# Second feed-forward down projection: seven half-depth products for each block of two token tiles and two column blocks, in place of eight

## The chip, the cores and the metric

The kernel runs on one core of one Trainium2 chip. The metric is the device time of one execution in microseconds (us); lower is better. All data is float32, and each float32 matmul of the program stands in the trace as two records on TensorE (PE), so 704 matmuls are 1408 records.

## The reference, cut to what matters

The program is a two-layer block with a modulation vector, two kinds of mixers and a convolved feed-forward network. The change touches only the feed-forward network of the second layer (`l = 1`), where the context rows are no longer needed and 512 tokens are left:

```
D_MODEL = 1024
SEQ = 512
D_FF = ((8 * D_MODEL // 3 + 127) // 128) * 128        # 2816, 22 tiles of 128

def conv_ffn(h, w_up, conv_w, w_down):
    a, g = jnp.split(dwconv(h @ w_up, conv_w), 2, axis=-1)
    return (jax.nn.silu(g) * a) @ w_down

x = x + mx[:, :, 5] * rmsnorm(conv_ffn(hx, ffn_w_up[l], ffn_conv[l], ffn_w_down[l]), norm_g[l, 3])
```

The product `(silu(g) * a) @ w_down` is the down projection: 512 tokens by 2816 hidden rows by 1024 columns. After it come the norm of each token's row, the gate and the addition to `x`, and `x` is the output.

## The kernel before

The kernel is written engine by engine: each stage is a block with one program for each engine, and the engines wait for each other by semaphores. There is no scheduler, so the order of the calls in the source is the order on the engine. At the end of a block all engines meet at a barrier (its instructions carry the line of the `with ... nc.Block()`, L1369 for `mix_and_up`). The last two stages are `mix_and_up(c, 1, 0, "cd_out", ...)`, which ends with the up projection, and `down_and_store(c)`.

**Up projection.** The hidden rows are made in 22 pairs (a gate tile and a value tile of 128 hidden rows each). Pairs 2 to 21 are made with seven products of half depth (`UpPairs`), and each goes through DVE (VectorE) in one iteration of the loop over `n`: `join_weights(n + 1)` makes four sums of the next pair's weights (L1639 to L1644), two `convolve` calls finish the pair before (L362, L366), seven additions gather the seven products (L1648, from PSUM), and `multiply(n - 1)` forms the finished hidden tile (L1617). After the loop, DVE still convolves and multiplies pair 21. ACT (ScalarE) copies, scales and takes the silu. `hidden[:, n, :]` holds 768 columns for each tile, of which the second layer uses 512.

**Down projection.** `Down` runs 32 units: for two groups of token tiles, (0, 1) and (2, 3), for eight column blocks of 128, for the two tiles of the group. A unit (L1916) is 22 matmuls with a hidden tile as the stationary operand and 128 columns of weights as the moving one, summed in one PSUM bank of 128 columns. ACT copies the even units out (L1937) and DVE the odd ones (L1943); ACT squares each (L1957). At the half DVE sums the squares of tiles 0 and 1 (L1822), ACT takes the root (L1826), and DVE divides, gates and adds these rows (L1833, L1835, L1838); at the end the same is done for tiles 2 and 3.

**Weights.** All weights come through a ring of four slots, filled by SP (SyncE) in the order of `c.plan`. A load waits until the products that used its slot are done (`c.used`). For the down projection each column block takes two slots, the upper and the lower half of the 2816 rows (11 tiles of 128 columns), so that two column blocks are in the ring at a time. The first four loads are issued by the stage before.

Of the kernel before, what the change touches and what calls it, by code (L numbers as in the profile page):

```python
# [326 lines left out]
def plan_all(c):  # L327
# [1015 lines left out]
def mix_and_up(c, l, z, name, src):  # L1343
# [25 lines left out]
    with st, nc.Block() as block:  # L1369
# [6 lines left out]
        strassen, copied, whole, weights_joined, tokens_joined = \  # L1376
            (sem(n) for n in ("strassen", "copied", "whole", "weights_joined", "tokens_joined"))

        @block.sync
        def _(sp):  # L1380
# [180 lines left out]
        def _(dve):  # L1561
# [106 lines left out]
            for n in range(begun, FT):  # L1668
# [62 lines left out]
def ffn_hidden(c):  # L1731
    return c.arena[:, 0:FT * N_ALL].rearrange("p (k t) -> p k t", k=FT), FT * N_ALL
# [504 lines left out]
                nc.vector.tensor_copy(v_[:, t, :], c.ps[:, (0, 2, 4, 5)[t % 4], 0:128]).then_inc(v_dve, 1)  # L2237


def down_and_store(c):  # L2240


    nc = c.nc
    st, sem = stage(c)
    rows = RowChain(c, sem, Down.CHUNKS)
    down = Down(c, 1, [(0, 1), (2, 3)], sem, rows)
    n_units, half = len(down.units), len(down.units) // 2
    with st, nc.Block() as block:
        @block.sync
        def _(sp):  # L2250
            c.stream(sp, "down1")
            for t in range(TX):
                sp.wait_ge(rows.added, t + 1)
                sp.dma_start(c.a["out"][0, t * 128:(t + 1) * 128, :], c.x[:, t, :]).then_inc(c.stored, 16)
            sp.wait_ge(c.stored, 16 * TX)

        @block.tensor
        def _(pe):
            for n in range(n_units):
                down.unit(pe, n)  # L2260

        @block.scalar
        def _(act):
            for n in range(n_units):
                if n % 2 == 0:
                    down.keep_act(act, n)
                if n:
                    down.square(act, n - 1)
                if n == half + 1:
                    for i in range(2):  # L2270
                        rows.branch_root(act, i)
            down.square(act, n_units - 1)
            for i in range(2, TX):
                rows.branch_root(act, i)

        @block.vector
        def _(dve):
            for n in range(n_units):
                if n == half:
                    for i in range(2):  # L2280
                        rows.sum_squares(dve, i, half)
                if n == half + 2:
                    for i in range(2):
                        rows.add(dve, i)
                if n % 2:
                    down.keep_dve(dve, n)
            for i in range(2, TX):
                rows.sum_squares(dve, i, n_units)
            for i in range(2, TX):
                rows.add(dve, i)  # L2290

# [1068 lines left out]
```

## Time and profile before

| | |
|---|---|
| median of three runs | 2490.5 us (2490.29 to 2492.77) |
| the profiled execution | 2486.43 us, of which the span of its instructions is 2484.6 us |
| PE busy | 2269.7 us, 91% of the span |
| DVE busy | 1112.6 us, 45% |
| ACT busy | 546.1 us, 22% |
| L1916, both down projections | 405.2 us of PE, 3520 records |
| the second down projection | from 2315.30 us, for 159.65 us, 1408 records |

Times in the rows count from the start of the span. A matmul's record has a duration that overlaps with the next one's, so the pace of PE is read from distances between events and not from durations. "PEclk" or the number before the DMA share in a row of windows is the granted clock of TensorE: 1.00 is 2.4 GHz and 0.50 is 1.2 GHz. "Idle before <-releaser" says how long an engine stood before an instruction and what ended that.

### The profile page before, as it was taken

What the parts mean: (1) busy time and instruction counts of PE and PEld (TensorE: products, weight loads), DVE (VectorE), ACT (ScalarE), POOL (GpSimd) and SP (SyncE); (2) the same over time, 40 slices, a digit from 0 to 9 for tenths busy, and PEclk for the clock granted to TensorE, in tenths of its full rate; (3) what the DMA queues carried; (4) which work ended last, traced back from release to release, by engine and by line L of the source; (5) the groups of instructions that cost most, each with busy time, mean ns of one, the idle gap of its engine ahead of it and who ended that gap; (6) DMA issues with size and microseconds to landing.
All of it is one profiled execution on the core that took longest, in us unless ns stands there. A gap on an engine that the chain in (4) does not pass through costs nothing. (4 is left out here: it accounts for less than half of the span.)

```text
span 2484.6 us, 39011 instructions
## 1 busy us (share of the span) xinstructions
PE 2269.7 (91%) x16786; PEld 1677.7 (68%) x16786; DVE 1112.6 (45%) x2140; ACT 546.1 (22%) x1241; POOL 229.9 (9%) x303
## 2 busy tenths in 40 slices
PE   3999989979993999999989999998887899999998
PEld 1557655558882865555559999545454588888898
DVE  2124822257761255666660003232676536677211
ACT  3102722321212231111110002111452132111110
POOL 2000100027760000000000000000210000000000
PEclk9999989989996999999999999999798899999999
DMA  8351001000003012122134556411000213333454
GB/s 327 113 192 35 1 18 51 0 1 4 4 4 136 5 47 68 51 63 56 52 80 151 160 168 202 142 60 27 29 1 18 68 35 85 85 85 85 126 155 128
DMA packets 236301, 193.55 MB, mean 78 GB/s; under 512 B 5395, under 2 KB 220130, under 8 KB 235938
## 3 DMA queue, kind: packets, MB, share of 16 engines
q1 hardware_dynamic: 223266, 145.53, 20.3%
q0 software_dynamic: 11776, 42.27, 4.8%
q8 instruction: 133, 2.18, 0.4%
q10 hardware_dynamic: 1088, 3.26, 0.3%
q14 instruction: 38, 0.31, 0.0%
HBM read 188.94 MB, written 2.10 MB: 77 GB/s over the span
## 5 line engine op out<-in xcount | busy, mean ns | idle before, releaser
L1454 PE MATMUL banks<-mem 128*128 128x384 f32 (+1 forms) x2296 | 622.1, 433 | 0.0
L1454 PEld LDWEIGHTS banks<-mem 128*128 128x128 f32 x2296 | 434.3, 189 | 187.3
L1916 PE MATMUL banks<-mem 128*128 128x128 f32 x3520 | 405.2, 277 | 13.9 <-PEq L1369 12.6
L1916 PEld LDWEIGHTS banks<-mem 128*128 128x128 f32 x3520 | 400.6, 194 | 23.7 <-issue 22.4
L2001 PE MATMUL banks<-mem 128*128 128x512 f32 x400 | 191.4, 609 | 6.0 <-issue 6.0
L1943 DVE COPY mem<-banks 128x128 f32<-128x128 f32 x40 | 11.7, 293 | 350.5 <-PE banks L1916 350.4
L1394 PE MATMUL banks<-mem 128*128 128x256 f32 x640 | 143.2, 384 | 13.2 <-PEq L616 11.1
L1648 DVE TENSOR_TENSOR mem<-mem,banks 128x384 f32<-128x384 f32 (+1 forms) x287 | 131.1, 487 | 38.5 <-PE banks L1454 35.7
L1394 PEld LDWEIGHTS banks<-mem 128*128 128x128 f32 x640 | 122.6, 193 | 32.1 <-issue 14.0
L921 PE MATMUL banks<-mem 64*64 64x64 f32 x3840 | 127.4, 220 | 18.5 <-DVE mem L1197 11.4
L921 PEld LDWEIGHTS banks<-mem 64*64 64x64 f32 x3840 | 119.7, 136 | 28.8 <-DVE mem L1197 13.7
L697 PE MATMUL banks<-mem 128*128 128x512 f32 x256 | 130.9, 592 | 1.2 <-PEq L415 1.2
L2001 PEld LDWEIGHTS banks<-mem 128*128 128x128 f32 x400 | 76.3, 194 | 76.1 <-issue 70.8
L1524 ACT ACTIVATE mem<-mem 128x768 f32<-128x768 f32 (+1 forms) x44 | 32.5, 739 | 342.4 <-DVE mem L366 342.4
L362 DVE SCALAR_TENSOR_TENSOR mem<-banks,mem 128x511 f32<-128x511 f32 (+1 forms) x44 | 28.0, 663 | 172.0 <-ACT mem L726 107.5
L1639 DVE TENSOR_TENSOR mem<-mem 128x512 f32<-128x512 f32 x41 | 28.4, 694 | 168.1 <-DMA mem<-in_ffn_w_up 168.1
L1533 ACT ACTIVATE mem<-mem 128x768 f32<-128x768 f32 (+1 forms) x82 | 66.0, 829 | 145.5 <-DVE mem L1648 145.5
L1937 ACT ACTIVATE mem<-banks 128x128 f32<-128x128 f32 x40 | 11.1, 278 | 362.3 <-PE banks L1916 350.2
L698 PEld LDWEIGHTS banks<-mem 128*128 128x128 f32 x256 | 48.4, 189 | 61.7 <-issue 61.7
L366 DVE SCALAR_TENSOR_TENSOR mem<-mem 128x511 f32<-128x511 f32 x124 | 78.2, 659 | 2.9
L362 DVE SCALAR_TENSOR_TENSOR mem<-mem 128x511 f32<-128x511 f32 x124 | 77.9, 657 | 0.5 <-ACT mem L1533 0.5
L698 PE MATMUL banks<-mem 128*128 128x256 f32 x256 | 76.2, 378 | 0.0
(343 smaller groups left out, 2743.9 us busy)
## 6 DMA issues: line engine op xcount, KB each, us to landing
mem<-in_ffn_w_up SPq DMA_DIRECT2D x88, 512.0 KB, 4.3
mem<-in_ffn_w_down SPq DMA_DIRECT2D x64, 704.0 KB, 6.6
mem<-in_w_mod POOLq DMA_DIRECT2D x40, 1024.0 KB, 7.5
mem<-in_ab_w_in SPq DMA_DIRECT2D x14, 1024.0 KB, 5.3
mem<-in_w_mod SPq DMA_DIRECT2D x8, 1024.0 KB, 14.1
mem<-in_cd_w_in SPq DMA_DIRECT2D x8, 1024.0 KB, 5.6
mem<-in_ab_w_out SPq DMA_DIRECT2D x4, 1024.0 KB, 9.0
mem<-in_cd_w_out SPq DMA_DIRECT2D x4, 1024.0 KB, 9.0
```

What stands on the lines that cost most here:

```text
L362: step = v.scalar_tensor_tensor(out[:, 1:n], src[:, 0:n - 1], tap(0), out[:, 1:n], ALU.mult, ALU.add)
L366: step = v.scalar_tensor_tensor(out[:, 0:n - 1], src[:, 1:n], tap(2), out[:, 0:n - 1], ALU.mult, ALU.add)
L697: nc.tensor.matmul(c.ps[:, x, :], w[:, k, :], ht[:, k, 0:N_X], start=k == 0, stop=k == KT - 1)
L698: last = nc.tensor.matmul(c.ps[:, z, 0:N_Z], w[:, k, :], ht[:, k, N_X:N_ALL], start=k == 0, stop=k == KT - 1)
L921: last = mm(c.ps[pa, LEVEL[i], fr], lhs[pa, fr], rhs[pa, fr], start=True, stop=True)
L1394: last = nc.tensor.matmul(c.ps[:, unit_banks[n % 4], 0:256], src[:, k, t * 128:(t + 1) * 128], w[:, k, :], start=k == 0, stop=k == KT - 1)
L1454: last = nc.tensor.matmul(fast.out(i, name), weights[:, k, :], tokens[:, k, :], start=k == 0, stop=k == 3)
L1524: f(gbuf[:, 0:n_all], gbuf[:, 0:n_all], ACT.Silu).then_inc(gated, 1)
L1533: f(dst[:, 0:n_all], fast.raw(n, half), ACT.Identity, scale=middle_tap(n, half)).then_inc(drained, 1)
L1648: v.tensor_tensor(to, one, fast.out(i, name), ALU.add).then_inc(whole, 1)
L1916: last = c.nc.tensor.matmul(c.ps[:, n % self.n_banks, 0:128], hidden[:, k, t * 128:(t + 1) * 128], w, start=k == 0, stop=k == FT - 1)
L2001: last = c.nc.tensor.matmul(c.ps[:, self.bank(n)[0], :], w[:, k, :], ht[:, k, 0:N_X], start=k == 0, stop=k == KT - 1)
```

## The change

`down_and_store` uses a new class `DownPairs` in place of `Down`. Its unit of work is a step: two token tiles (a group) by two column blocks of 128. For the four 128x128 blocks of the output it makes seven products instead of eight, each over half of the 22 hidden tiles (11), from sums of blocks of the hidden rows and sums of blocks of the weights. There are eight steps, four for each group. A step has two parts, of 6 and 5 of the 11 tiles, and a part's weights take two slots of the ring: now 256 columns wide and 6 or 5 tiles deep. Part by part, DVE makes the four weight sums (`join`), PE runs the seven products (`step`), and after the second part ACT keeps the first product (`keep_first`) and DVE adds up the others (`gather`). ACT takes four squares for each step. The sums of the hidden rows (`join_hidden`) are made in the stage before, 44 operations of 256 columns on DVE, as the hidden tiles arise.

```diff
-    c.plan("down1", down(a["ffn_w_down"][1]) * 2)
+    c.plan("down1", [ktiles(a["ffn_w_down"][1])[:, 11 * h + lo:11 * h + hi, i:i + 256]
+                     for i in range(0, D, 256) for lo, hi in DownPairs.PARTS for h in range(2)] * 2)
...
+            def join_hidden(n):
+                k = n - FT // 2
+                if z == 0 and k >= 0:
+                    (a11, a21), (a12, a22) = (DownPairs.tokens(c, row) for row in (k, n))
+                    s1, s2, s4 = DownPairs.sums(c, k)
+                    dve.wait_ge(done, n + 1)
+                    v.tensor_tensor(s1, a21, a22, ALU.add).then_inc(hidden_joined, 1)
+                    dve.wait_ge(hidden_joined, 4 * k + 1)
+                    v.tensor_tensor(s2, s1, a11, ALU.subtract).then_inc(hidden_joined, 1)
+                    v.tensor_tensor(a21, a11, a21, ALU.subtract).then_inc(hidden_joined, 1)
+                    dve.wait_ge(hidden_joined, 4 * k + 2)
+                    v.tensor_tensor(s4, a12, s2, ALU.subtract).then_inc(hidden_joined, 1)
...
                 add_up(i, value_rows[0], value_rows[0], "p4")
+                join_hidden(n - 1)
             convolve_pair(FT - 1, 0)
             convolve_pair(FT - 1, 1)
             multiply(FT - 1)
+            join_hidden(FT - 1)
...
+class DownPairs:
+    PARTS = ((0, 6), (6, 11))
+    ORDER = ("p1", "p2", "p6", "p5", "p7", "p3", "p4")
+    FREED = {"p6": 1, "p2": 2, "p7": 3, "p5": 5, "p3": 6, "p4": 7}
+    STEPS, PER_GROUP = 8, 4
...
+        for q in range(2 * self.STEPS):
+            for h in range(2):
+                c.used[self.lo + 2 * q + h] = (self.product, 7 * q + 7)
...
+    def join(self, dve, q):
+        v = self.c.nc.vector
+        b11, b12, b21, b22, t1, t2, t4 = self.parts(q)
+        for h in range(2):
+            self.c.arrived(dve, self.lo + 2 * q + h)
+        v.tensor_tensor(t1, b12, b11, ALU.subtract).then_inc(self.joined, 1)
+        dve.wait_ge(self.joined, 4 * q + 1)
+        v.tensor_tensor(t2, b22, t1, ALU.subtract).then_inc(self.joined, 1)
+        v.tensor_tensor(b12, b22, b12, ALU.subtract).then_inc(self.joined, 1)
+        dve.wait_ge(self.joined, 4 * q + 2)
+        v.tensor_tensor(t4, b21, t2, ALU.subtract).then_inc(self.joined, 1)
...
+    def step(self, pe, s):
...
+            def times(name, rows, weights):
+                if s and part == 0:
+                    if name == "p1":
+                        pe.wait_ge(self.copied, s)
+                    else:
+                        pe.wait_ge(self.whole, 7 * (s - 1) + self.FREED[name])
+                for k in range(lo, hi):
+                    last = c.nc.tensor.matmul(self.out(name), rows(k)[:, group, :], weights[:, k - lo, :],
+                                              start=k == 0, stop=k == 10)
+                last.then_inc(self.product, 1)
+
+            for h in range(2):
+                c.arrived(pe, self.lo + 2 * q + h)
+            times("p1", lambda k: self.tokens(c, k)[0], b11)
+            times("p2", lambda k: self.tokens(c, 11 + k)[0], b21)
+            pe.wait_ge(self.joined, 4 * q + 2)
+            times("p6", lambda k: self.sums(c, k)[1], t2)
+            times("p5", lambda k: self.sums(c, k)[0], t1)
+            pe.wait_ge(self.joined, 4 * q + 4)
+            times("p7", lambda k: self.tokens(c, k)[1], b12)
+            times("p3", lambda k: self.sums(c, k)[2], b22)
+            times("p4", lambda k: self.tokens(c, 11 + k)[1], t4)
...
+    def keep_first(self, act, s):
+        act.wait_ge(*self.done(s, "p1"))
+        self.c.nc.scalar.activation(self.place(s, 0, 0), self.out("p1"), ACT.Copy).then_inc(self.copied, 1)
+
+    def gather(self, dve, s):
+        y11, y12, y21, y22 = (self.place(s, b, j) for b in range(2) for j in range(2))
+
+        def add_up(to, one, name):
+            dve.wait_ge(*self.done(s, name))
+            self.c.nc.vector.tensor_tensor(to, one, self.out(name), ALU.add).then_inc(self.whole, 1)
+
+        dve.wait_ge(self.copied, s + 1)
+        add_up(y12, y11, "p6")
+        add_up(y11, y11, "p2")
+        dve.wait_ge(self.whole, 7 * s + 1)
+        add_up(y21, y12, "p7")
+        dve.wait_ge(self.whole, 7 * s + 3)
+        add_up(y22, y21, "p5")
+        add_up(y12, y12, "p5")
+        dve.wait_ge(self.whole, 7 * s + 5)
+        add_up(y12, y12, "p3")
+        add_up(y21, y21, "p4")
...
         @block.scalar
         def _(act):
...
+            for s in range(steps):
+                down.keep_first(act, s)
+                if s == half:
                     for i in range(2):
                         rows.branch_root(act, i)
+                down.square(act, s)
...
         @block.vector
         def _(dve):
...
+            down.join(dve, 0)
+            for s in range(steps):
+                down.join(dve, 2 * s + 1)
+                if s == half:
                     for i in range(2):
+                        rows.sum_squares(dve, i, 4 * half)
                     for i in range(2):
                         rows.add(dve, i)
+                down.gather(dve, s)
+                if s + 1 < steps:
+                    down.join(dve, 2 * s + 2)
```

On DVE, the end of the up projection reads as follows before the change: the last seven additions of pair 21 (L1648, around one L1617 for pair 20), then the convolution and the product of pair 21, and then the barrier.

```order
L1648 TENSOR_TENSOR mem<-mem,banks 128x256 x2
L1617 TENSOR_TENSOR mem<-mem 128x512
L1648 TENSOR_TENSOR mem<-mem,banks 128x256 x5
L362 SCALAR_TENSOR_TENSOR mem<-mem 128x511
L366 SCALAR_TENSOR_TENSOR mem<-mem 128x511
L362 SCALAR_TENSOR_TENSOR mem<-mem 128x511
L366 SCALAR_TENSOR_TENSOR mem<-mem 128x511
L1617 TENSOR_TENSOR mem<-mem 128x512
```

After the change DVE has, at the same place (all lines of this function stand one later), two groups of four sums of hidden rows, L1665 to L1670:

```order
L1649 TENSOR_TENSOR mem<-mem,banks 128x256 x5
L1665 TENSOR_TENSOR mem<-mem 128x256
L1667 TENSOR_TENSOR mem<-mem 128x256
L1668 TENSOR_TENSOR mem<-mem 128x2x128
L1670 TENSOR_TENSOR mem<-mem 128x256
L363 SCALAR_TENSOR_TENSOR mem<-mem 128x511
L367 SCALAR_TENSOR_TENSOR mem<-mem 128x511
L363 SCALAR_TENSOR_TENSOR mem<-mem 128x511
L367 SCALAR_TENSOR_TENSOR mem<-mem 128x511
L1618 TENSOR_TENSOR mem<-mem 128x512
L1665 TENSOR_TENSOR mem<-mem 128x256
L1667 TENSOR_TENSOR mem<-mem 128x256
```

The first group, for hidden tile 20, stands ahead of the last convolutions; the second, for tile 21, stands behind the last product and ahead of the barrier.

On DVE, in the middle of the down projection, the program before the change has nothing but copies around the rows of tiles 0 and 1:

```order
L1943 COPY mem<-banks 128x128 x8
L1822 TENSOR_REDUCE mem<-mem 128x1 x2
L1943 COPY mem<-banks 128x128
L1833 RECIPROCAL mem<-mem 128x1
L1835 SCALAR_TENSOR_TENSOR mem<-mem 128x1024
L1838 TENSOR_TENSOR mem<-mem 128x1024
```

After the change the rows of tiles 0 and 1 (L1840 to L1856) stand in step 4, between the weight sums of its second part (640 columns) and its `gather` (L2360), and the weight sums for step 5 (768 columns, L2304 on) stand behind both:

```order
L2309 TENSOR_TENSOR mem<-mem 128x640
L1840 TENSOR_REDUCE mem<-mem 128x1 x2
L1851 RECIPROCAL mem<-mem 128x1
L1853 SCALAR_TENSOR_TENSOR mem<-mem 128x1024
L1856 TENSOR_TENSOR mem<-mem 128x1024
L1851 RECIPROCAL mem<-mem 128x1
L1853 SCALAR_TENSOR_TENSOR mem<-mem 128x1024
L1856 TENSOR_TENSOR mem<-mem 128x1024
L2360 TENSOR_TENSOR mem<-mem,banks 128x128 x7
L2304 TENSOR_TENSOR mem<-mem 128x768
L2306 TENSOR_TENSOR mem<-mem 128x768
L2307 TENSOR_TENSOR mem<-mem 128x6x128
```

On PE the last stage is one kind of instruction, before and after, with fewer of them:

```order
-L1916 MATMUL banks<-mem 128x128 x704
+L2328 MATMUL banks<-mem 128x128 x616
```

Shape and operands of a matmul stay as they were.

## Rows read from the trace of the kernel before

**Rows 1.** The page's first line.

```profile
span 2484.6 us, 39011 instructions
```

**Rows 2.** Chain of waits that ended last: start us, us, what.

```profile
2315.30 159.65 PE banks L1916 x1408
...
2474.97 0.30 DVE mem L1943
...
2480.34 1.23 DVE mem L1838
```

**Rows 3.** Timeline of the down projection: start us, us, engine, line, operation.

```profile
2322.66 0.28 ACT L1937 ACTIVATE mem<-banks 128x128 f32<-128x128 f32 x1 [8.56 <-PE banks L1916]
...
2337.40 0.29 DVE L1943 COPY mem<-banks 128x128 f32<-128x128 f32 x1 [9.53 <-PE banks L1916]
```

**Rows 4.** Timeline where the up projection ends.

```profile
2269.70 40.37 PE L1454 MATMUL banks<-mem 128*128 128x256 f32 x186
...
2310.11 0.42 DVE L1648 TENSOR_TENSOR mem<-mem,banks 128x256 f32<-128x256 f32 x1 [1.24 <-PE banks L1454]
2310.45 0.75 DVE L362 SCALAR_TENSOR_TENSOR mem<-mem 128x511 f32<-128x511 f32 x1
...
2314.13 0.69 DVE L1617 TENSOR_TENSOR mem<-mem 128x512 f32<-128x512 f32 x1 [0.70 <-ACT mem L1524]
```

**Rows 5.** Windows there: us, busy PE, PEld, DVE, ACT, POOL, clock, DMA share, GB/s.

```profile
2313.00:2313.50 0.50, 0.00 (x0) 0.00 (x0) 0.43 (x1) 0.04 (x1) 0.00 (x0) 0.53 1.15 349
...
2319.50:2320.00 0.50, 0.50 (x4) 0.50 (x4) 0.00 (x0) 0.00 (x0) 0.00 (x0) 0.64 0.00 0
```

**Rows 6.** DVE groups by shape: count, busy us, mean ns of one, idle before.

```profile
L1648 DVE TENSOR_TENSOR mem<-mem,banks 128x256 f32<-128x256 f32 x140 | 53.5, 419 | 4.4 <-PE banks L1454 3.1
...
L1641 DVE TENSOR_TENSOR mem<-mem 128x512 f32<-128x512 f32 x41 | 28.4, 694 | 1.4
...
L1617 DVE TENSOR_TENSOR mem<-mem 128x768 f32<-128x768 f32 x22 | 21.1, 960 | 0.9 <-ACT mem L1524 0.9
```

**Rows 7.** Timeline of one iteration of the up projection, on DVE.

```profile
2279.67 0.69 DVE L1639 TENSOR_TENSOR mem<-mem 128x512 f32<-128x512 f32 x1 [3.12 <-DMA mem<-in_ffn_w_up]
...
2286.50 1.99 DVE L1648 TENSOR_TENSOR mem<-mem,banks 128x256 f32<-128x256 f32 x5
...
2291.70 0.69 DVE L1639 TENSOR_TENSOR mem<-mem 128x512 f32<-128x512 f32 x1 [3.20 <-DMA mem<-in_ffn_w_up]
2292.43 0.69 DVE L1641 TENSOR_TENSOR mem<-mem 128x512 f32<-128x512 f32 x1
2293.03 0.69 DVE L1642 TENSOR_TENSOR mem<-mem 128x512 f32<-128x512 f32 x1
```

**Rows 8.** Timeline of the rows' roots, at the half and at the end.

```profile
2402.35 1.28 ACT L1826 ACT_TABLE_LOAD   x1
...
2476.16 0.17 DVE L1833 RECIPROCAL mem<-mem 128x1 f32<-128x1 f32 x1 [0.20 <-ACT mem L1826]
```

**Rows 9.** A pair of weight loads: issue, windows; and all 28 loads of the stage.

```profile
2327.56 10.88 SPq L191 DMA_DIRECT2D mem<-in_ffn_w_down  x4
...
2333.00:2333.50 0.50, 0.50 (x7) 0.50 (x6) 0.00 (x0) 0.41 (x3) 0.00 (x0) 1.00 1.23 296
2333.50:2334.00 0.50, 0.50 (x7) 0.50 (x6) 0.00 (x0) 0.04 (x1) 0.00 (x0) 1.00 0.77 179
...
DMA to landing us min/median/max: 4.5/5.9/7.7
```

**Rows 10.** Two short stands of PE in the timeline, and windows behind them.

```profile
1482.79 3.50 PE L1916 MATMUL banks<-mem 128*128 128x128 f32 x18 [1.23 <-DVE mem L1759]
...
1483.50:1487.00 3.50, 3.50 (x20) 3.50 (x19) 0.00 (x0) 0.00 (x0) 0.00 (x0) 0.51 1.17 323
...
908.22 1.13 PE L1413 MATMUL banks<-mem 128*128 128x256 f32 x4 [2.12 <-ACT mem L1504]
...
906.00:910.00 4.00, 1.88 (x9) 1.60 (x9) 3.68 (x8) 2.17 (x7) 0.00 (x0) 1.00 0.02 4
```

More of the change, by code:

```diff
@@ L2237, in _, with __init__, tokens, sums @@
                 nc.vector.tensor_copy(v_[:, t, :], c.ps[:, (0, 2, 4, 5)[t % 4], 0:128]).then_inc(v_dve, 1)
+class DownPairs:
[3 more added lines that the diff above has]
+    STEPS, PER_GROUP = 8, 4
+    def __init__(self, c, sem, rows):
+        self.c, self.rows = c, rows
+        self.lo = c.range_of["down1"][0]
+        names = ("down_product", "down_copied", "down_whole", "down_joined")
+        self.product, self.copied, self.whole, self.joined = (sem(n) for n in names)
+        self.room = c.arena[:, FT * N_ALL:FT * N_ALL + 2 * 3 * 768].rearrange("p (b s n) -> p b s n", b=2, s=3)
+        for q in range(2 * self.STEPS):
+            for h in range(2):
+                c.used[self.lo + 2 * q + h] = (self.product, 7 * q + 7)
+    @staticmethod
+    def tokens(c, row):
+        pairs = ffn_hidden(c)[0][:, row, 0:N_X].rearrange("p (g b t) -> p g b t", g=2, b=2)
+        return pairs[:, :, 0, :], pairs[:, :, 1, :]
+    @staticmethod
+    def sums(c, k):
+        hidden = ffn_hidden(c)[0]
+        z = c.z.rearrange("p t d -> p (t d)")
+        o = _TABLE["cos"][0] + 256 * (k - 8)
+        last = z[:, 256 * k:256 * k + 256] if k < 8 else c.table[:, o:o + 256]
+        return [ap.rearrange("p (g t) -> p g t", g=2) for ap in (hidden[:, k, N_X:N_ALL], hidden[:, FT // 2 + k, N_X:N_ALL], last)]
+    def parts(self, q):
+        lo, hi = self.PARTS[q % 2]
+        n = hi - lo
+        (b11, b12), (b21, b22) = ([self.c.slot(self.lo + 2 * q + h, n, 256)[:, :, at:at + 128] for at in (0, 128)] for h in range(2))
+        t1, t2, t4 = (self.room[:, q % 2, s, 0:128 * n].rearrange("p (k n) -> p k n", k=n) for s in range(3))
+        return b11, b12, b21, b22, t1, t2, t4
+    def join(self, dve, q):
[9 more added lines that the diff above has]
+        v.tensor_tensor(t4, b21, t2, ALU.subtract).then_inc(self.joined, 1)
+    def out(self, name):
+        return self.c.ps[:, self.ORDER.index(name), 0:128]
+    def step(self, pe, s):
+        c, group = self.c, s // self.PER_GROUP
+        for part in range(2):
+            q = 2 * s + part
+            lo, hi = self.PARTS[part]
+            b11, b12, b21, b22, t1, t2, t4 = self.parts(q)
+            def times(name, rows, weights):
[19 more added lines that the diff above has]
+            times("p4", lambda k: self.tokens(c, 11 + k)[1], t4)
+    def place(self, s, b, j):
+        at = 256 * (s % self.PER_GROUP) + 128 * j
+        return self.rows.y[:, 2 * (s // self.PER_GROUP) + b, at:at + 128]
+    def done(self, s, name):
+        return self.product, 14 * s + 7 + self.ORDER.index(name) + 1
+    def keep_first(self, act, s):
[17 more added lines that the diff above has]
+        add_up(y21, y21, "p4")
+    def square(self, act, s):
+        for n, (b, j, ready) in enumerate(((0, 0, 2), (1, 1, 4), (0, 1, 6), (1, 0, 7)), 4 * s):
+            t, chunk = 2 * (s // self.PER_GROUP) + b, 2 * (s % self.PER_GROUP) + j
+            act.wait_ge(self.whole, 7 * s + ready)
+            if n:
+                act.wait_ge(self.rows.squared, n)
+            self.c.nc.scalar.activation(self.rows.junk, self.place(s, b, j), ACT.Square,
+                                        accum_out=self.rows.squares[:, t, chunk:chunk + 1]).then_inc(self.rows.squared, 1)
@@ L2245, in down_and_store @@
     rows = RowChain(c, sem, Down.CHUNKS)
-    down = Down(c, 1, [(0, 1), (2, 3)], sem, rows)
-    n_units, half = len(down.units), len(down.units) // 2
+    down = DownPairs(c, sem, rows)
+    half, steps = down.PER_GROUP, down.STEPS
     with st, nc.Block() as block:
@@ L2258, in _ @@
         def _(pe):
-            for n in range(n_units):
-                down.unit(pe, n)
+            for s in range(steps):
+                down.step(pe, s)
         @block.scalar
         def _(act):
[L2264 to L2269, printed above, removed]
+            for s in range(steps):
+                down.keep_first(act, s)
+                if s == half:
                     for i in range(2):
                         rows.branch_root(act, i)
-            down.square(act, n_units - 1)
+                down.square(act, s)
             for i in range(2, TX):
```

13 lines of the change are left out of this document (4 added, 9 removed).

## The prediction, made before the changed kernel ran

> **What bounds the kernel now.** I read the chain of waits first. Its last long piece is the whole second down projection: PE runs 1408 records from 2315.30 us for 159.65 us with nothing between them, and behind it stands a tail on DVE and ACT that ends at 2481.57 us [rows 2]. The span is 2484.6 us [rows 1]; the profiled execution took 2486.43 us and the median of the runs is 2490.5 us, so the profile lies 4.1 us below the median. The sum below is made on the profiled execution, and I carry the difference over to the median.
>
> Then the timeline inside the stage. DVE is idle for 9.53 of 9.83 us before each of its copies and ACT for 8.56 us before its first one, in both cases for PE [rows 3]. So PE sets the time of the stage and work taken from it is worth its whole length, as long as the new work on DVE does not make PE wait.
>
> The pace: DVE's copies at 2337.40 us [rows 3] and 2474.97 us [rows 2] are 28 units of 44 records apart, 137.57 / 1232 = 111.7 ns a record. The first unit took 7.36 us (2315.30 to 2322.66 [rows 2, 3]) where 44 records at that pace take 4.91 us: 2.45 us more. The reason is in the windows: PE stopped at 2269.70 + 40.37 = 2310.07 us [rows 4], the granted clock fell to its 1.2 GHz level soon after 2313.0 us, and came back to 2.4 GHz within 2319.5 to 2320 us [rows 5].
>
> **PE, removed.** 704 matmuls become 616, 88 fewer, or 176 records of the same shape. 176 x 111.7 ns = 19.65 us. Is the pace the same when PE changes bank and product every 5 or 6 matmuls and not every 22? The up projection changes every 4: its iterations start 12.03 us apart [rows 7] with 7 x 4 x 2 = 56 records of 256 columns, 214.8 ns each. Twice 111.7 would be 223. So changing products costs nothing that shows. I count **-19.65 us**. Its bounds are that price and, if each of the 112 products cost one more record's 0.11 us, 12 us less; the row of the up projection is near and excludes most of that.
>
> **DVE prices.** A 256-column TENSOR_TENSOR from PSUM takes 419 ns, one of 512 columns 694, of 768 columns 960 [rows 6]: 1.04 ns a column, so 640 columns take 827 and 256 from SBUF about 430. Starts lie 0.73 us apart where the second needs the first, 0.60 where it does not [rows 7]: the length plus 0.04, or less 0.09. A join of 768 columns then has its second sum ready after 1.00 + 0.96 = 1.96 us, and all four after 3.7 us. Four sums of hidden rows take 0.47 + 0.34 + 0.34 + 0.43 = 1.58 us, or move the next instruction by 1.49 us.
>
> **Sums of hidden rows.** Of the 11 groups, 9 stand at the end of an iteration of the up projection. DVE is idle there, for 3.12 and 3.20 us before `join_weights`, for the weights [rows 7]; 1.49 us fit, and cost nothing. Without that cover it would be up to 9 x 1.49 = 13.4 us. The last two have none. PE's last product ends at 2310.07 us; from its addition at 2310.11 us DVE works through the convolutions to the product at 2314.13 us, which ends at 2314.82 us [rows 4]; PE starts 0.48 us later [rows 2]. The group for tile 20 stands ahead of these convolutions (+1.49 us), the one for tile 21 behind the product (+1.58 us). **+3.07 us**, bounds 2.5 (nothing between sums) and 4. PE then stands 8.3 us instead of 5.2; the clock is down before it restarts either way, and I leave the 2.45 us as they are, bounds 1.7 and 3.2.
>
> **Start of the stage.** The first four loads are issued by the stage before, as now. DVE's first join has its second sum ready 1.96 us after the barrier; PE needs it after two products of 6 matmuls, 2.68 us at full clock and later at the low one. Nothing.
>
> **Each boundary between steps.** A part of 6 takes PE 7 x 6 x 0.2233 = 9.38 us, one of 5 7.82 us, a step 17.19 us. Let a step end at T. The last addition of `gather` needs the last product, so it starts at T + 0.02; the join of the next part 0 stands behind it, starts at about T + 0.23 (128 columns take 0.29, from L1943 [rows 3], less 0.09) and has its second sum at T + 2.19. PE asks for it at T + 2.68. The margin is 0.5 us, and all of the join that PE waits for is behind work that can't end before T. The third and fourth sums are there at T + 3.9 and PE asks at T + 5.4. The second part's join has 9.4 us. Nothing, but thinly.
>
> **Loads.** 32 loads and 22.5 MB, as before. A part-0 pair grows from 1.44 to 1.57 MB and is issued when the same slots' products end, with only the part of 5 (7.82 us) as cover; before, the cover was two units, 9.83 us. The pair issued at 2327.56 us flowed until about 2334.0 us, 6.4 us, at up to 296 GB/s; 0.13 MB more is 0.45 us more, so 6.9 us. That is 0.9 us ahead of PE, and ahead of DVE. The longest of the 28 loads took 7.7 us [rows 9]; with 0.45 us added that one would be 0.3 us late. Nothing, upper bound 1 us.
>
> **Step 4.** Here DVE has the rows of tiles 0 and 1 ahead of `gather`, and they wait for ACT's roots, which stand behind `keep_first(4)`, and this waits for p1 of the second part: 9.38 + 1.12 = 10.50 us after the step's start. Then the copy (0.3), the table load (1.28 [rows 8]) and the root with its way to DVE (0.23): 12.31 us. From there the two rows take DVE as long as at the end, from 2476.16 us [rows 8] to 2480.34 + 1.23 [rows 2], 5.41 us: 17.72 us, when the step itself is over at 17.19. `gather` follows (seven additions of 128 columns, two of them held by the one before: 5 x 0.21 + 2 x 0.33 = 1.7 us, the first with a head start of 0.09), then the join: its second sum is ready at 17.72 - 0.09 + 1.7 + 1.96 = 21.3 us, and PE asks for it at 17.19 + 2.68 = 19.87. PE stands **+1.45 us** once (bounds 0.8 and 2.5). What is queued behind on DVE, the join of step 5's second part, has 9 us; the others are not late.
>
> **The clock after that.** A short stand can cost more than itself. At 1482.79 us PE had stood 1.23 us, and in the next 3.5 us the clock was 0.51; at 908.22 us it had stood 2.12 us and the clock stayed at 1.00 [rows 10]. Near in place and kind is the first (dense 128-column matmuls before and after), so I take the fall: 3.3 us at half pace, **+1.65 us**; the other bound is 0. The Trainium skill bears on this (TensorE: Matmul & The Clock Gate, "HAM oscillation — how this bites in real kernels"): it warns only of idle gaps longer than this one. By it the sum would lose this term, -15.2 us and not -13.5; the row at 1482.79 us speaks against it, that at 908.22 us for it.
>
> **Tail.** Behind the last product stand an addition of 128 columns, one square, and then the same sums, roots and rows as now: the addition takes the place of the copy of 0.30 us. Nothing.
>
> **Sum.** -19.65 + 3.07 + 1.45 + 1.65 = -13.5 us. The profiled execution goes from 2486.4 to 2472.9 us, and the median from 2490.5 to **2477.0 us**, 0.54% less. A measurement of this kernel can tell about 0.2%, 5 us, from no change.
>
> **The rivals.**
>
> *The stand in step 4 does not lower the clock, or does not come about.* A stand of 1.45 us passes, and PE goes on at full pace: 2475.4 us; without the stand too, 2473.9. For it: the row at 908.22 us [rows 10]. Chance 0.2. The section of the Trainium skill's TensorE page named above would have it so.
>
> *The margins at the boundaries are not there.* If the second sum or the load is late by 0.3 to 1 us at six further boundaries, PE stands there each time: 2 to 6 us, 2479 to 2483 us. For it: the margin is 0.5 us of a 1.96 us chain, priced from other shapes. Against: 768 columns have a row of their own. Chance 0.18.
>
> *Stands that take the clock with them, slower than before.* The same place, but the join is late by 1.2 us or more, the length that took the clock at 1482.79 us: each of six boundaries then costs 1.23 + 1.65 us, 17.3 us, and the median is 2477.0 + 17.3 = 2494 us. It decides from a join's second sum 1.7 us later than priced. Nothing in the rows makes a 768-column sum so slow. Chance 0.03.
>
> *The gap in the up projection is not free.* If DVE's idle time there were needed, the nine groups would cost 13.4 us and the result be 2490 us, no change. Against: DVE waits for weights and has the join ready long before PE's next iteration. Chance 0.04.
>
> **How the numbers follow.** The forecast has 0.55, with its own range of 2475.5 to 2479 us from the bounds of the stage's start and of the stand. The range for 8 in 10 takes in the first two rivals: 2472.5 to 2483 us. Faster by over 0.2% are the forecast and the first two rivals, 0.93, less a little for what I don't see: 0.91. Same 0.05, slower 0.04.
>
> **What would show it.** In the changed kernel: L2328 with 1232 records and 137.6 us plus 2.4 for the clock plus 3.1; PE's first record of the stage near 2318.4 us; DVE's joins starting 0.2 us after each eighth of the stage; one idle time of 1.4 us of PE, for the DVE line L2306, some 91 us after the stage's start, and a clock of 0.5 behind it; DVE's idle time before L1640 down from 3.2 to 1.7 us in the iterations from 12 on. Wrong would be: PE idle at every step for L2306 or for a load, iterations of the up projection longer than 12.03 us, or records of L2328 further apart than 111.7 ns.

## The result, and the profile after

The changed kernel took 2462.39 us (median of 4 runs, 2459.82 to 2465.93), the kernel before 2490.39 us in the same sitting (4 runs, 2489.77 to 2492.77): a ratio of 0.9887, interval 0.987 to 0.9904, 28 us less. The forecast was 13.5 us less, 2477 us, with a range down to 2472.5. Four later sittings of the same two kernels, on three chips and with many more runs, gave another size:

| sitting | kernel before, median (runs) | changed, median (runs) | ratio, interval |
|---|---|---|---|
| first | 2490.39 (4) | 2462.39 (4) | 0.9887, 0.987 to 0.9904 |
| c_after, chip 11 | 2481.19 (23) | 2464.60 (6) | 0.9941, 0.9923 to 0.9959 |
| c_after_2, chip 3 | 2478.42 (16) | 2462.01 (6) | 0.9932, 0.9908 to 0.9956 |
| c_after_3, chip 11 | 2481.37 (23) | 2466.34 (6) | 0.9928, 0.9905 to 0.995 |
| c_after_4, chip 13 | 2477.91 (19) | 2467.71 (8) | 0.9941, 0.9917 to 0.9965 |

Single executions of the kernel before lay between 2469.94 and 2492.78 us, those of the changed one between 2458.98 and 2473.88 us in the four later sittings. The four later ratios have a mean of 0.9936, 16 us. A ratio here is not the quotient of the two medians beside it (for c_after_4 that would be 0.9959).

Here are the page's first line and the group of the new matmuls, to stand beside [rows 1].

```profile
span 2461.2 us, 38845 instructions
...
L2328 PE MATMUL banks<-mem 128*128 128x128 f32 x1232 | 139.9, 277 | 9.5 <-PEq L1370 8.3
```

The span is 23.4 us shorter than that of before. The chain of waits, to stand beside [rows 2] (start us, us, what):

```profile
2310.45 81.08 PE banks L2328 x710
...
2391.86 1.28 ACT L1844
...
2393.59 1.30 DVE mem L1853
...
2402.34 49.19 PE banks L2328 x438
...
2456.92 1.23 DVE mem L1856
```

The down projection is still PE's, but in one place the chain leaves it: in step 4 it goes over ACT's table load and DVE's rows of tiles 0 and 1. PE's last record ends at 2402.34 + 49.19 = 2451.53 us, and the tail behind it takes 6.62 us, as before. The timeline where the up projection ends answers to [rows 4]:

```profile
2302.18 0.42 DVE L1649 TENSOR_TENSOR mem<-mem,banks 128x256 f32<-128x256 f32 x1 [1.24 <-PE banks L1455]
2302.52 0.42 DVE L1665 TENSOR_TENSOR mem<-mem 128x256 f32<-128x256 f32 x1
...
2303.99 0.75 DVE L363 SCALAR_TENSOR_TENSOR mem<-mem 128x511 f32<-128x511 f32 x1
...
2307.66 0.69 DVE L1618 TENSOR_TENSOR mem<-mem 128x512 f32<-128x512 f32 x1 [0.70 <-ACT mem L1525]
2308.39 0.43 DVE L1665 TENSOR_TENSOR mem<-mem 128x256 f32<-128x256 f32 x1
...
2310.45 34.73 PE L2328 MATMUL banks<-mem 128*128 128x128 f32 x295 [8.31 <-PEq L1370]
```

The addition at 2302.18 us is the first thing behind PE's last product, as that at 2310.11 us was in [rows 4]. Four sums then move the convolutions by 1.47 us, four more stand ahead of the barrier, and PE stands 8.31 us where it stood 5.22. From the end of PE's last record of the up projection (2302.14 us) to the end of its last of the down projection it is 149.4 us; before it was 2474.97 - 2310.07 less the 0.02 us to DVE's start, 164.9 us. **So this stretch gives 15.5 us in this pair of profiles, and the other 7.9 us lie in front of it, where the change only adds the sums of the hidden rows on DVE.** Windows of the same stages of both kernels show where. First the kernel before, 26.6, 256.4, 92.3, 59.7 and 275.9 us long (clock is the third number from the end):

```profile
1593.10:1619.70 26.60, 21.73 (x54) 10.85 (x54) 7.46 (x17) 4.20 (x10) 0.00 (x0) 0.88 0.15 47
1619.70:1876.10 256.40, 232.10 (x1070) 127.02 (x1070) 131.13 (x326) 78.79 (x178) 25.24 (x24) 0.91 0.08 25
1882.20:1974.50 92.30, 73.37 (x208) 42.57 (x208) 65.73 (x80) 9.39 (x16) 4.95 (x4) 0.85 0.17 57
1974.50:2034.20 59.70, 59.13 (x272) 51.12 (x272) 13.24 (x29) 17.00 (x56) 0.00 (x0) 0.97 0.10 27
2034.20:2310.10 275.90, 273.70 (x1264) 238.86 (x1264) 190.32 (x348) 55.39 (x103) 0.00 (x0) 0.99 0.31 84
```

Then the changed kernel:

```profile
1597.40:1620.90 23.50, 18.58 (x55) 8.67 (x55) 7.54 (x17) 4.21 (x10) 0.00 (x0) 1.00 0.17 54
1620.90:1874.70 253.80, 226.83 (x1071) 124.60 (x1071) 131.69 (x326) 78.62 (x178) 25.43 (x24) 0.93 0.09 26
1880.70:1970.00 89.30, 70.39 (x209) 40.68 (x209) 65.70 (x80) 9.38 (x16) 4.95 (x4) 0.89 0.18 59
1970.00:2028.00 58.00, 57.45 (x272) 49.93 (x273) 13.24 (x29) 17.04 (x56) 0.00 (x0) 1.00 0.10 28
2028.00:2302.10 274.10, 271.97 (x1264) 237.64 (x1264) 203.13 (x383) 55.27 (x103) 0.00 (x0) 1.00 0.31 85
```

Each stage is 1.7 to 3.1 us shorter, 12.2 us together, each with a higher granted clock and the same work of the other engines, except that DVE has the new sums in the last one (383 instructions in place of 348). An earlier stage (from 227.3 to 331.3 us before, 227.8 to 335.1 us after) went the other way, by 3.2 us, with a clock of 0.92 before and 0.87 after; the stages not shown give back the rest. The two theories for this: **A**, chance decides in each execution which of PE's short stands are followed by a stretch at 1.2 GHz; **B**, something in the build makes the early stages of the changed kernel faster. The experiments decide this first, and then take the prediction's terms one by one.

### The profile page after: what moved, and what is told of

It is laid out like the page before. It is cut to its first block and busy times, and to the rows that moved or that the text cites. A ratio compares the mean times of both kernels' runs of the same rounds, so it can differ in the third digit from the quotient of the medians.

```text
span 2461.2 us, 38845 instructions
## 1 busy us (share of the span) xinstructions
PE 2239.3 (91%) x16610; PEld 1650.8 (67%) x16610; DVE 1192.6 (48%) x2288; ACT 545.8 (22%) x1233; POOL 229.9 (9%) x303
## 5 line engine op out<-in xcount | busy, mean ns | idle before, releaser
L1455 PEld LDWEIGHTS banks<-mem 128*128 128x128 f32 x2296 | 434.2, 189 | 187.4
L1934 PE MATMUL banks<-mem 128*128 128x128 f32 x2112 | 245.7, 277 | 8.9 <-PEq L1370 7.4
L1934 PEld LDWEIGHTS banks<-mem 128*128 128x128 f32 x2112 | 241.2, 194 | 18.3 <-issue 17.0
L1395 PE MATMUL banks<-mem 128*128 128x256 f32 x640 | 141.6, 381 | 13.2 <-PEq L617 11.1
L2328 PE MATMUL banks<-mem 128*128 128x128 f32 x1232 | 139.9, 277 | 9.5 <-PEq L1370 8.3
L2328 PEld LDWEIGHTS banks<-mem 128*128 128x128 f32 x1232 | 139.3, 193 | 10.2 <-issue 8.9
L1395 PEld LDWEIGHTS banks<-mem 128*128 128x128 f32 x640 | 121.4, 191 | 31.6 <-issue 14.0
L2019 PEld LDWEIGHTS banks<-mem 128*128 128x128 f32 x400 | 75.4, 192 | 75.1 <-issue 69.8
L699 PEld LDWEIGHTS banks<-mem 128*128 128x128 f32 x256 | 48.4, 189 | 61.7 <-issue 61.7
## 6 DMA issues: line engine op xcount, KB each, us to landing
mem<-in_w_mod SPq DMA_DIRECT2D x8, 1024.0 KB, 14.9
```

Of the source, the lines that this page charges most:

```text
L699: last = nc.tensor.matmul(c.ps[:, z, 0:N_Z], w[:, k, :], ht[:, k, N_X:N_ALL], start=k == 0, stop=k == KT - 1)
L1395: last = nc.tensor.matmul(c.ps[:, unit_banks[n % 4], 0:256], src[:, k, t * 128:(t + 1) * 128], w[:, k, :], start=k == 0, stop=k == KT - 1)
L1455: last = nc.tensor.matmul(fast.out(i, name), weights[:, k, :], tokens[:, k, :], start=k == 0, stop=k == 3)
L1934: last = c.nc.tensor.matmul(c.ps[:, n % self.n_banks, 0:128], hidden[:, k, t * 128:(t + 1) * 128], w, start=k == 0, stop=k == FT - 1)
L2019: last = c.nc.tensor.matmul(c.ps[:, self.bank(n)[0], :], w[:, k, :], ht[:, k, 0:N_X], start=k == 0, stop=k == KT - 1)
L2328: last = c.nc.tensor.matmul(self.out(name), rows(k)[:, group, :], weights[:, k - lo, :], start=k == 0, stop=k == 10)
```

## The experiments

"Stage" below is always the time from the end of PE's last record of the up projection to the end of its last record of the down projection. It is the sum of the stand (the time in which PE waits) and the down projection.

### The same kernels again: c_before, c_before_2, c_before_3, c_after, c_after_2, c_after_3, c_after_4

No edit; each gave a further profile and a sitting of its own or with others.

> The kernel before once more, unchanged, for a second profile. Outside the last two stages the traces of before and after differ by 7.9 us although their instructions there are the same. Theory A (chance: short stands of TensorE lower its clock in one execution and not in another): ratio 1.000, but the profile has another number of stretches at the lower clock than 24, and its upstream stages differ by several us from those of the first profile, in either direction. Theory B (something in the build makes the early stages of the changed kernel faster): ratio 1.000 and the same stretches and stage lengths as in the first profile, within 1 us.

> The changed kernel once more, unchanged. Theory A: its stages ahead of the last up projection differ from those of its first profile by several us, and the ratio moves within 0.985 to 0.992. Theory B: they repeat within 1 us, and the ratio is 0.9887 again. Both: the stretch from TensorE's last record of the up projection to its last record of the down projection is 149.4 us again, 15.5 less than before (within 2 us, for the clock).

> The changed kernel once more, beside the kernel before on the same chip. Theory A (the median of one sitting holds a part that has nothing to do with the change: how often short stands lower TensorE's clock): a third ratio between 0.987 and 0.996, and again a last stage that ends 148 to 152 us after the up projection's last record. Theory B (the change is worth the 28 us of the first sitting): 0.9887 again.

> The kernel before once more, as a control beside the others of this call. Ratio 1.000. Its level tells whether the 2490 us of the first sitting comes back: by theory A its executions spread over 2470 to 2490 us; by theory B they lie at 2490 us.

> The changed kernel, a fourth sitting. By the stages measured so far (15.0 us less in the last two) the ratio is 0.9940, with its interval around that; by the first sitting 0.989.

> The kernel before, unchanged. Theory A: 2470 to 2491 us, median 2478 to 2482, and the time ahead of the down projection grows by about half of TensorE's busy time at the lower clock. If the level of 2490 us belongs to a chip, a sitting on such a chip shows it again.

> The changed kernel, unchanged. Theory A: 2459 to 2474 us, 15 to 16 us below the kernel before of the same sitting (ratio 0.9935). If a chip lifts the kernel before to 2490 us and not this one: 0.989.

The kernel before against itself gave 1.0002, 0.9979 (interval 0.996 to 0.9998, so two samples of one kernel can differ by 0.2% and look clear) and 1.0003. The ratios of the changed kernel are in the table above. The stages:

| profile | stand + down projection | stage, us |
|---|---|---|
| before, first profile | 5.22 + 159.65 | 164.9 |
| c_before, _2, _3 | 5.22 + 158.91, 159.31, 158.90 | 164.1, 164.5, 164.1 |
| changed, first profile | 8.31 + 141.08 | 149.4 |
| c_after, _2, _3, _4 | 8.28 + 141.05, 141.53, 141.51, 141.05 | 149.3, 149.8, 149.8, 149.3 |

The means are 164.4 and 149.5 us: the change takes **14.9 us** out of this stretch, and any profile of the one kernel against any of the other gives 14.3 to 15.5 us. What varies lies ahead of them: PE's last record of the up projection ends between 2293.9 us (c_before_2) and 2311.0 us (c_after), and the changed kernel alone has both 2297.7 and 2311.0. I added up the time in which PE was busy at the lower clock ahead of that point. In the 16 profiles of all kernels here it goes from 79 to 122 us, and the end of the up projection follows it: a straight line with 0.39 us for each us fits them with 1.0 us of spread around it (correlation 0.98), and kernels before and changed lie on the same line. Half a us for each us would be the price of the halved clock alone. The same instructions show it directly. In the kernel before, its first profile:

```profile
1770.50:1780.70 10.20, 10.20 (x43) 6.27 (x42) 5.96 (x17) 4.05 (x10) 2.53 (x2) 0.51 0.00 0
```

In the first profile of the changed kernel, at the same place in the program:

```profile
1770.00:1780.00 10.00, 8.11 (x62) 5.20 (x62) 8.82 (x23) 4.57 (x11) 3.63 (x3) 1.00 0.00 0
```

And the stand of 1.23 us at 1482.79 us, which [rows 10] show with a clock of 0.51 behind it, in c_after:

```profile
1484.00:1487.00 3.00, 2.61 (x54) 1.74 (x52) 1.61 (x5) 0.00 (x0) 0.71 (x1) 1.00 0.30 73
1487.00:1492.00 5.00, 4.16 (x37) 4.16 (x38) 1.15 (x9) 0.00 (x0) 0.00 (x0) 1.00 1.16 325
```

There the clock stays at 2.4 GHz. Over all 16 profiles, at the same PE record each time: the stand of 1.23 us is followed by the lower clock in 14 and not in c_before_2 and c_after; the stretch of 10.2 us near 1770 us comes in 5, among them kernels before and changed; the stand of 2.12 us at 908.22 us [rows 10] is followed by the lower clock in one alone, e1_root_first. Theory B falls: the changed kernel's early stages did not repeat, and the kernel before can be faster there than it. Theory A holds for the variation, in the sense that the same instructions get either clock; what decides it in an execution is not shown. One thing it does not cover: all four runs of the first sitting of the kernel before lay at 2489.8 us or more, and of its 117 runs in the later sittings only 6 did. Why that sitting was so even, and so high, stays open; its chip is not on record, and the three later chips did not show its level.

### ACT's roots first: e1_root_first

```diff
             for s in range(steps):
-                down.keep_first(act, s)
                 if s == half:
                     for i in range(2):
                         rows.branch_root(act, i)
+                down.keep_first(act, s)
                 down.square(act, s)
```

> The changed kernel with ACT's roots of tiles 0 and 1 ahead of its copy of step 4's first product, not behind it. If step 4's stand of 1.1 us comes from the rows waiting for the roots: no idle time of TensorE for L2306 any more, last stage 1.1 us shorter (2.7 with a fall of the clock that it may cause). If it comes from the join alone: unchanged.

Stage 8.28 + 140.32 = 148.6 us, 0.9 less than the mean of the changed kernel; ratio 0.994 (0.9923 to 0.9957) beside 0.9941 for c_after, which can't tell it. The wait for the join is gone, but another stand has its place, as PE's and DVE's rows of its timeline show:

```profile
2392.43 0.16 DVE L1851 RECIPROCAL mem<-mem 128x1 f32<-128x1 f32 x1 [0.20 <-ACT mem L1844]
...
2400.47 9.73 PE L2328 MATMUL banks<-mem 128*128 128x128 f32 x85 [0.69 <-issue]
2400.47 0.96 DVE L2304 TENSOR_TENSOR mem<-mem 128x768 f32<-128x768 f32 x1 [0.36 <-DMA mem<-in_ffn_w_down]
```

The roots now come in time. PE and DVE both start at 2400.47 us, DVE for the weights: this pair of 1.57 MB had been issued at 2391.99 us, 8.5 us earlier, and its cover is 7.8 us. The cause of the first stand is shown to be the order on ACT. That the load is what stands behind it is read from DVE's row, and no run moved the load. By the starts of the steps the removed stand had cost 1.70 us and the new one costs 0.86 (the step ahead of it takes 18.05 us, an undisturbed one 17.20), which makes up the 0.9.

### Only the sums of the hidden rows: e2_hidden_sums

```diff
                 add_up(i, value_rows[0], value_rows[0], "p4")
+                join_hidden(n - 1)
             convolve_pair(FT - 1, 0)
             convolve_pair(FT - 1, 1)
             multiply(FT - 1)
+            join_hidden(FT - 1)
```

> The kernel before with the sums of the hidden rows added on DVE and nothing else of the change. Its down projection reads hidden tiles 0 to 10 with half their token tiles replaced by a difference, so its output isn't the reference's. By the prediction's step: TensorE's stand ahead of the down projection goes from 5.2 to 8.3 us, the iterations of the up projection stay at 12.03 us, total +3.1 us (ratio 1.0012). If the sums in the iterations are not covered: up to +13 us more. If the early stages of a build vary by chance by several us, the total can come out on either side, and only the stage tells.

The stand went from 5.22 to 8.28 us, stage 167.3 us, 2.9 more than the kernel before. The ratio, 1.0003 (0.9987 to 1.0018), can't tell that. The sums inside the iterations are covered, in the timeline of this kernel:

```profile
2264.80 0.42 DVE L1669 TENSOR_TENSOR mem<-mem 128x256 f32<-128x256 f32 x1
2266.88 0.69 DVE L1639 TENSOR_TENSOR mem<-mem 128x512 f32<-128x512 f32 x1 [1.66 <-DMA mem<-in_ffn_w_up]
...
2279.09 0.69 DVE L1639 TENSOR_TENSOR mem<-mem 128x512 f32<-128x512 f32 x1 [1.93 <-DMA mem<-in_ffn_w_up]
```

DVE still waits 1.66 to 1.93 us for weights, where [rows 7] had 3.12 and 3.20. And PE's last ten iterations of the up projection, counted over 56 records each, start 12.11 us apart in this kernel, in the kernel before and in the changed one.

### The last two groups late: e3_sums_late

```diff
-                join_hidden(n - 1)
+                if n < FT - 1:
+                    join_hidden(n - 1)
...
-            join_hidden(FT - 1)
...
             down.join(dve, 0)
+            for i in range(2):
+                down.join_tokens(dve, i)
```

`join_tokens` makes the same four sums, for hidden tiles 20 and 21; PE waits for them ahead of p6 of the second part of step 0.

> The changed kernel with the last two groups of hidden sums (for tiles 20 and 21) made in the down projection behind its first join and not ahead of the barrier; TensorE waits for them ahead of the second part's p6. By the prediction's step the stand ahead of the down projection goes from 8.3 to 5.2 us, and nothing else is late: 3.1 us less from the up projection's last record to the down projection's last. A rival: the second part waits for them, and part of it comes back as a stand at p6.

The stand is 5.22 us, the down projection 141.36 us, stage 146.6 us, 2.9 less than the changed kernel, and nothing comes back at p6. Ratio 0.9929 (0.9902 to 0.9956) beside 0.9932 for c_after_2.

### TensorE kept busy at the seam: e4_warm

```diff
                 times("p4", value_w[:, 4:8], fast.t4)
+            if z == 0:
+                pe.wait_ge(whole, 7 * (FT - begun - 1))
+                spare = fast.out(FT - begun, "p1")
+                for k in range(18):
+                    nc.tensor.matmul(spare, c.tab["ident"], fast.b11[:, k % 4], start=True, stop=True)
```

> The changed kernel with 18 matmuls of 256 columns into a bank that is free, whose results nobody reads, behind the up projection's last product: TensorE is busy for 7.7 of the 8.3 us in which it stood. If the clock falls there for want of work: clock 1.00 throughout the down projection's start, its first 94 products of the first part at full pace, stage 1.6 us shorter. If the clock is lowered for another reason: the fall stays, and nothing is gained.

The windows at the seam and behind it:

```profile
2309.50:2318.00 8.50, 8.25 (x39) 6.88 (x37) 6.89 (x14) 1.39 (x3) 0.00 (x0) 1.00 0.48 154
2318.00:2322.00 4.00, 3.74 (x33) 3.77 (x34) 3.79 (x5) 0.00 (x0) 0.00 (x0) 1.00 0.00 0
```

The clock does not fall, and the down projection takes 139.52 us where the changed kernel took 141.05 to 141.53: 1.5 to 2.0 us, the price of the low clock at the start. In the medians it is not to be seen: 2469.27 us is 7.3 us above that of c_after_2 in the same sitting, with intervals that overlap (0.9947, 0.9927 to 0.9966).

### All three: e5_all, e5_all_2

> Three edits on the changed kernel together: the last hidden sums late, 11 matmuls in what is left of the stand, and ACT's roots ahead of its copy in step 4. By the prices: -3.1, -1.6 and -1.1 (or -2.7 where the clock fell) us, 5.8 us less than the changed kernel from the up projection's last record to the down projection's last, 143.6 us. The ratio to the kernel before about 0.992 where the changed kernel has 0.994.

> The kernel with all three edits again, for a second interval. By its first profile 143.9 us from the up projection's last record to the down projection's last against 149.5 of the changed kernel: ratio 0.9917 where the changed kernel has 0.9940.

Stages 5.22 + 138.69 and 5.22 + 138.63: 143.9 us both times, 5.6 us less than the changed kernel, against 5.8 expected. Here too one late load is left: PE stands 0.62 and 0.56 us ahead of step 4, where DVE waits for its weights as well. Ratios 0.9919 (0.9895 to 0.9943) and 0.9909 (0.9882 to 0.9935). Its stages are the shortest of the study. Its medians, 2458.01 and 2460.82 us, lie 4.0 and 5.5 us below those of the changed kernel in the same sittings (c_after_2 and c_after_3); the intervals overlap.

### The join later by 1.7 us: e6_late_join

```diff
                 if s + 1 < steps:
+                    idle = c.gates[:, 0].rearrange("p u d -> p (u d)")[:, 0:1536]
+                    nc.vector.tensor_tensor(idle, idle, idle, ALU.add)
                     down.join(dve, 2 * s + 2)
```

> The changed kernel with one more DVE operation of 1536 columns ahead of the first part's join at every boundary between steps; what it writes nobody reads. It takes 1.67 us, start to start. The prediction's margin there is 0.5 us, so TensorE should stand 1.2 us at six boundaries and 2.8 to 3.1 us after step 4: 10 us more. If each such stand also lowers the clock for 3.4 us, 7 x 1.7 = 12 us on top. If the margin is larger than computed, less than 8 us.

PE's timeline has a stand at each boundary (the fifth line is the one behind step 4):

```profile
2376.83 17.46 PE L2328 MATMUL banks<-mem 128*128 128x128 f32 x154 [1.23 <-DVE mem L2306]
2395.53 17.46 PE L2328 MATMUL banks<-mem 128*128 128x128 f32 x154 [1.24 <-DVE mem L2306]
2416.09 18.99 PE L2328 MATMUL banks<-mem 128*128 128x128 f32 x154 [3.10 <-DVE mem L2306]
```

The stands come where the prediction has its thin margin, and PE idles for 1.23 us against 1.2 computed and 3.10 against 2.8 to 3.1. That the figures meet is in part luck. A record lasts 0.275 us and the next one starts 0.112 us after it, so T, the end of a step's last record, lies 0.16 us behind the first start of the next step, and a stand counted from an end to a start leaves out as much. From start to start PE is late by 1.51 - 0.11 = 1.40 us, and 1.67 - 1.40 leaves a margin of 0.27 us. The first profile of the changed kernel says the same. The second weight sum of step 1,

```profile
2330.67 0.96 DVE L2306 TENSOR_TENSOR mem<-mem 128x768 f32<-128x768 f32 x1
```

ends at 2331.63 us and PE's first record that needs it starts at 2331.95 us; where PE waits for it (in e6_late_join) it starts 0.05 us behind the end. **The margin is 0.27 us, not 0.5.** The down projection took 153.77 us, 12.3 more than c_after_3 of the same sitting, and the ratio was 0.9989 (0.9971 to 1.0008): one operation of 1.7 us in the wrong place takes back 12.3 of the 14.9 us. Each step now takes 17.46 + 1.23 = 18.69 us where 17.20 us passed from one step to the next. Of the 0.26 us that this is more than the stand, 0.16 us is the overlap of records just named, and 0.10 us is left as the cost of starting again. The clock, in windows behind a stand of 1.23 us and behind that of 3.10 us:

```profile
2339.00:2343.00 4.00, 3.56 (x31) 3.56 (x32) 2.13 (x3) 0.00 (x0) 0.00 (x0) 1.00 0.58 197
...
2415.00:2418.50 3.50, 2.40 (x11) 2.41 (x12) 3.46 (x5) 0.00 (x0) 0.00 (x0) 0.63 0.22 75
```

## Why the prediction was right and wrong

**The pace (-19.65 us): right.** Undisturbed steps of 154 records start 17.20 us apart in the changed kernel, 111.7 ns a record, as before, and the change of product costs nothing. (49.19 us for 438 records would be 112.3 ns, but that stretch holds the restart behind the stand and the last record's whole length.)

**Sums of the hidden rows (+3.07): right.** 3.09 us in the first profile, 3.06 in e2_hidden_sums, and gone again in e3_sums_late. The sums in the iterations are free, as read from DVE's idle time.

**The start of the stage (left as it was): somewhat off.** In the first profiles the lower clock there cost 2.2 us before (159.65 us less 1408 records at 111.7 ns and the last record's overlap) and 1.6 us in the changed kernel (its first step takes 18.82 us). Over all profiles of the two kernels it cost 1.4 to 2.2 and 1.6 to 2.1 us. The bounds of 1.7 and 3.2 us held the forecast's own term, but 0.6 us of the first pair's gain are from here.

**Boundaries: right that nothing is late, and thinner than computed.** In the first profile the last addition, the first sum and the second sum start at 2329.47, 2329.68 and 2330.67 us, which is T + 0.02, 0.23 and 1.22 with T = 2329.45, as forecast. But the prediction let PE ask at T + 2.68, as if the next step began at T; it began 0.17 us earlier. The margin was 0.27 us, as e6_late_join confirmed from the other side.

**Step 4 (+1.45): right in kind, 0.25 us small.** The stand for the join at L2306 was 1.14 us in the first profile and 1.44 in c_after (1.09 to 1.44 in the five), and e1_root_first took it away by the order on ACT. By the starts of the steps it cost 1.70 us in both: steps 4 and 5 took 17.43 and 18.67 us in the first, 17.20 and 18.90 in c_after, against twice 17.20.

**Loads: nearly.** The 28 loads of the stage took 4.4 to 7.4 us in the first profile. The bound of "0.3 us late" is the one that e1_root_first met, with 0.7 us, behind the stand in step 4 that had hidden it; e5_all and e5_all_2 met it ahead of step 4, with 0.62 and 0.56 us. So the loads are late now and then, inside the upper bound of 1 us.

**The clock after step 4 (+1.65): wrong.** No profile of the changed kernel has a fall there, in five of five, nor have e3_sums_late and e4_warm with stands of 1.44 and 1.43 us, nor the six stands of 1.23 us in e6_late_join; that of 3.10 us had one. The step was the choice of one row (the stand at 1482.79 us [rows 10]) as near in kind, "dense 128-column matmuls before and after". The timeline of the kernel before shows otherwise:

```profile
1477.83 1.73 PE L1916 MATMUL banks<-mem 128*128 128x128 f32 x14
1479.48 1.04 PE L305 MATMUL banks<-mem 128*2 128x256 f32 x16
1480.46 1.10 PE L1749 MATMUL banks<-mem 2*128 2x2 f32 x32
1482.79 7.48 PE L1916 MATMUL banks<-mem 128*128 128x128 f32 x50 [1.23 <-DVE mem L1759]
```

Between the dense matmuls and the stand there are 2.1 us of matmuls with an operand of only two rows or two columns. In step 4 the dense ones run right up to the stand. Whether this is what makes the difference no run tests. The rival "does not lower the clock", with 0.2, was the right one. It had the Trainium skill (TensorE: Matmul & The Clock Gate, "HAM oscillation — how this bites in real kernels") on its side, which warns only of longer gaps. Here the trace agrees with it in step 4, where 1.09 to 1.44 us passed, but not everywhere: the stand of 1.23 us at 1482.79 us was followed by a fall in 14 of 16 profiles.

**The sum for the stages:** -13.5 forecast, -14.9 measured; with the clock term left out it would have been -15.2. For the first pair the measured terms close: -19.65 + 3.09 + 1.70 - 0.6 = -15.5 us.

**The range and the total: wrong.** The step that failed is the one where I took over the runs' level, the median of 2490.5 us, as a fixed starting point, with "A measurement of this kernel can tell about 0.2%, 5 us, from no change" and a range made only from the bounds of the edited terms. The variation of everything ahead of the stage was put at nothing. The stages that the change doesn't touch move the total by some 17 us from one execution to the next, over the number of stretches at 1.2 GHz. The three runs shown lay within 2.5 us of each other, and their own profiled execution lay 4.1 us below them; I wrote that difference down and carried it along as a constant, where it may have been a sign of this variation. The later sittings put the change at 10 to 17 us between medians, and the forecast's ratio, 2477.0 / 2490.5 = 0.9946, lies in the interval of all four. Their medians of the changed kernel, 2462.0 to 2467.7 us, still lie below the range, since the kernel before stood there at 2478 to 2481 us and not at 2490.5. Of the first sitting's 28 us, 15 are shown to be from the stages. The other 13 are left over by subtraction, and why that sitting had them stays open.

## What to carry to other kernels

Read a change of under 1% in the trace, from one fixed event to another around the edit, and not in the total: here the stage repeated within 1 us while the total of one kernel moved by 15 to 23 us. A median of a few runs is not a level to forecast from until other sittings have repeated it. When an engine is given work behind another's last result, compute the time until the next request, from start to start, and keep it: 0.27 us was left here, and 1.7 us more at each boundary cost 12 of the 15 us gained. Work that must be done before a barrier but is needed only later belongs behind it (3 us here), and an engine that would stand at a barrier can be kept at work for the clock's sake (1.5 to 2 us).

## What the runs showed of the hardware

The same stand of TensorE, with the same instructions around it, was followed by the 1.2 GHz level in one execution and by 2.4 GHz in another: that of 1.23 us at 1482.79 us in 14 of 16 profiles, that of 2.12 us at 908.22 us in one of 16. In the down projection's dense 128-column matmuls single stands of 1.09 to 1.44 us, in seven profiles, and six stands of 1.23 us in an eighth never lowered it, one of 3.10 us did. A stand of 1.23 us inside that run of matmuls lengthened the step by 1.49 us, 0.16 of it because records overlap and 0.10 at the restart. And one pair of loads of 1.57 MB took 8.5 us from issue to use where the single loads of the stage had medians of 5.7 us (changed) and 5.9 us (before) to landing.
